# The values of two heads multiplied together on the two halves of the array's columns, with a second buffer of turned weights

## The chip, the cores and the metric

One core of one Trainium2 chip runs the whole kernel, one launch. The metric is the device time of that launch in microseconds (us). The profiled execution is another run of the same program; its own time is given beside the median below.

## What is computed

The reference is one inference step of a two-layer trunk: a gated-linear-attention layer, then a stick-breaking attention layer over shared K and V. It runs for a prompt of 512 tokens and for 8 samples of one token each with 2048 cached positions. What the change touches is the stick-breaking attention of the prompt (16 heads of 64 features), which stands late in the program. Beside it runs the sum over the cached values of the samples.

```python
# one head, a block of queries; k, v: the 512 new tokens
z = q @ k.T * scale + bias
mask = k_pos < q_pos
log_keep = where(mask, log_sigmoid(-z), 0)
later = cumsum(log_keep, reverse=True) - log_keep
a = where(mask, exp(log_sigmoid(z) + later), 0)
o = a @ v                      # then times silu(g), then the output projection
```

## The kernel before

Every engine has its own program written out by hand, and counting semaphores tie them together. The order on an engine is the order in which its block is written; a wait holds up all that stands behind it on that engine.

The stage of the prompt's heads starts at about 802 us and ends at about 949 us of the span. For head h the work runs through the engines like this:

- TensorE, `scores(h)` (L1762): four mask products and four score products into banks 1, 0 and 2; the rows of the array used are 64, the features of one head. It is issued one head ahead.
- ScalarE, `head_sigmoids(h)` (L865): two sigmoids of each bank into `pcum[h % 2]` and `psig[h % 2]`.
- VectorE, `head_products(h)` (L1300): four scans along the keys, then four multiplications. The result, the weights, stands in `psig[h % 2]`; semaphore `a_p`.
- TensorE, `weights_back(h)` (L1778): ten 128x128 transposes of the weights into banks 3, 4 and half of bank 1; semaphore `at_t`.
- VectorE, `head_weights(h)` (L1320): three copies of these banks into the buffer `pat`, the turned weights; semaphore `at_out`.
- TensorE, `values(h)` (L1792): four products of V with `pat`, 1280 columns in all, that fill only 64 of the array's 128 columns; heads of even number write partitions 0 to 63 of bank 5, odd ones 64 to 127; semaphore `o_p`.
- VectorE, `gate_pair(i)` (L1316): one multiplication of bank 5 by the gate, once for two heads; semaphore `u1_out`.

There is one buffer `pat`, so `head_weights(h)` waits for `values(h - 1)`. An fp32 product stands twice in the trace, as two passes.

Between these stands the work of the samples. The cached V has 128 pages of 512 KB. `value_quad(m0)` (L1804) multiplies four pages, each on 32 of the array's 128 columns; the stage holds quads 16 to 31, one for each head. After each fourth quad VectorE masks the sum (`sample_rows`, L1248, semaphore `ob`), TensorE turns it with eight products of one column (`sample_features`, L1820, semaphore `sf_mm`) and VectorE multiplies it in (`sample_gate`, L1256, semaphore `so1_used`). The next quad overwrites the same banks, so it waits for `so1_used`.

The pages are loaded by SyncE (`load_page`, L449). A page of V lies in slot `(n - FEW) % 7` of seven, n the page's number in the order of loading, so the slot of a page comes free when the quad that used the page seven before is done; SyncE waits for that on `v_used`, which counts quads. Of two quads that follow each other, 4 + 4 pages, the last page of the second one lies in the slot of the first page of the first one. It can be issued only when the first quad has ended.

The loop of TensorE at L1850 sets the order: for each head `scores(h + 1)`, `weights_back(h)`, then `value_quad` and `values(h)`; where a quad starts a new sample (h = 0, 4, 8, 12) it is `sample_features`, `values(h)`, `value_quad`.

Of the kernel before, what the change touches and what calls it, by code (L numbers as in the profile page):

```python
# [4 lines left out]
F32 = mybir.dt.float32  # L5
# [7 lines left out]
P = 128  # L13
D = 1024
KT = D // P
NP_TOK = 512
NS = 8
T = NP_TOK + NS
H2 = T // 2
TB = NP_TOK // P  # L20
# [7 lines left out]
SH, HD = 16, 64  # L28
# [60 lines left out]
QUAD = 4  # L89
# [14 lines left out]
NZ = P * (1 + 2 + 3 + 4)  # L104

AB = {0: (3, 0), 1: (4, 0), 3: (4, 384), 2: (1, 256)}
AO = {0: 0, 1: 512, 3: 896, 2: 1024}
# [54 lines left out]
PER_SAMPLE = NPG // QUAD  # L162
# [20 lines left out]
def build(nc, x_prompt, x_sample, state_gla, cache_k, cache_v, page_table, p_prompt, p_sample,  # L183
# [3 lines left out]
    with ExitStack() as ctx:  # L187
# [3 lines left out]
        def at(name, shape, dt, offset):  # L191
            return nc.alloc_sbuf_tensor_at(name, shape, dt, offset=offset)

        def size(shape, dt=F32):
            n = 2 if dt == BF16 else 4
            for s in shape[1:]:
                n *= s
            return (n + 63) // 64 * 64

        def new(name, shape, dt=F32):  # L200
            t = at(name, shape, dt, top[0])
            top[0] += size(shape, dt)
            assert top[0] <= nc.sbuf_usable_end, (name, top[0] - nc.sbuf_usable_end)
            return t
# [57 lines left out]
        offB = off_phase  # L262
# [40 lines left out]
        V1 = new("V1", [P, TB, D])  # L303
# [13 lines left out]
        pz = size([P, NZ + 4])  # L317
        psig = [at(f"psig{i}", [P, NZ], F32, offB + i * pz) for i in range(2)]
        pcum = [at(f"pcum{i}", [P, NZ + 4], F32, offB + (2 + i) * pz) for i in range(2)]
        pat = at("pat", [P, NZ], F32, offB + 4 * pz)  # L320
        w_unsplit = [w_raw[:, 0, :], w_raw[:, 1, :]] + [at(f"w_unsplit{i}", [P, 2048], F32, off_split + i * 8192)[:] for i in range(2)]

        pp = [ctx.enter_context(nc.psum_tensor(f"pp{i}", [P, 2, 512], F32)) for i in range(4)]
        bank = [pp[i // 2][:, i % 2, :] for i in range(8)]
# [9 lines left out]
        def S(name):  # L334
            if name not in sems:
                sems[name] = ctx.enter_context(nc.semaphore(name))
            return sems[name]
# [603 lines left out]
        def _(dve):  # L941
# [230 lines left out]
            for u in range(8):  # L1172
                h = u // 2
# [140 lines left out]
                last.then_inc(S("a_p"), 1)  # L1314

            def gate_pair(i):  # L1316
                dve.wait_ge(S("o_p"), 2 * i + 2)
                nc.vector.tensor_tensor(g1T[:, i, 0:NP_TOK], bank[5], g1T[:, i, 0:NP_TOK], ALU.mult).then_inc(S("u1_out"), 1)

            def head_weights(h):  # L1320

                dve.wait_ge(S("at_t"), h + 1)
                if h:
                    dve.wait_ge(S("o_p"), h)
                for bk, b0, c0, n in ((3, 0, 0, 512), (4, 0, 512, 512), (1, 256, 1024, 256)):
                    last = nc.vector.tensor_copy(pat[:, c0:c0 + n], bank[bk][:, b0:b0 + n])
                last.then_inc(S("at_out"), 1)

            head_products(0)
            for h in range(SH):  # L1330
                quad = 16 + h
                if quad % PER_SAMPLE == 0:
                    sample_rows(quad // PER_SAMPLE - 1)
                if h % 2 == 0 and h:
                    gate_pair(h // 2 - 1)
                head_weights(h)
                if quad % PER_SAMPLE == 0:
                    sample_gate(quad // PER_SAMPLE - 1)
                if h + 1 < SH:
                    head_products(h + 1)  # L1340
            gate_pair(SH // 2 - 1)
            sample_rows(NS - 1)
            sample_gate(NS - 1)
# [33 lines left out]
        def _(pe):  # L1377
# [150 lines left out]
            for k in range(KT):  # L1528
                if k >= 3:
                    pe.wait_ge(S("x_T"), k - 2)  # L1530
                for b in range(TB):
                    last = nc.tensor.transpose(bank[4 + k % 3][:, b * P:(b + 1) * P], xin[:, b, k * P:(k + 1) * P], ident[:])
# [8 lines left out]
            for k in range(KT):  # L1541
                last = nc.tensor.matmul(sB[0:SW, 336:336 + RANK], hsA[:, k % SV, SW * (k // SV):SW * (k // SV + 1)], wgk[:, k, :],
                                        start=(k == 0), stop=(k == KT - 1))
# [10 lines left out]
            for h in range(GH):  # L1554
                last = nc.tensor.matmul(sC[:, 384 + h * NS:384 + (h + 1) * NS], w2[:, h * P:(h + 1) * P], lrT[:, 0:NS],
                                        start=True, stop=True)
# [6 lines left out]
            for h in range(GH):  # L1563
                nc.tensor.matmul(bank[4 + h], w2[:, h * P:(h + 1) * P], sqacc[0:RANK, 0:NP_TOK],
                                 start=True, stop=True).then_inc(S("gk_mm"), 1)
# [120 lines left out]
            for u in range(8):  # L1686
                h = u // 2
# [74 lines left out]
            def scores(h):  # L1762

                i, r = h // 2, (h % 2) * HD
                for e, (bk, _, blocks) in enumerate(ZBANKS):
                    if h:
                        pe.wait_ge(S("sig_p"), (h - 1) * len(ZBANKS) + e + 1)
                    for q in blocks:
                        c0, n = ZB[q][1], (q + 1) * P
                        nc.tensor.matmul(bank[bk][:, c0 + n - P:c0 + n], identb[:], maskneg[:],  # L1770
                                         start=(q != 2), stop=False, skip_group_check=True)
                    for q in blocks:
                        c0, n = ZB[q][1], (q + 1) * P
                        last = nc.tensor.matmul(bank[bk][:, c0:c0 + n], q1T[r:r + HD, i, q * P:(q + 1) * P],  # L1774
                                                K1T[r:r + HD, i, 0:n], start=False, stop=True, skip_group_check=True)
                    last.then_inc(S("z_p"), 1)

            def weights_back(h):  # L1778

                pe.wait_ge(S("a_p"), h + 1)  # L1780
                if h:
                    pe.wait_ge(S("at_out"), h)
                for kb in (0, 1, 3, 2):
                    bk, c0 = AB[kb]
                    if bk == ZBANKS[0][0] and h + 1 < SH:
                        pe.wait_ge(S("sig_p"), (h + 1) * len(ZBANKS) + 1)
                    for q in range(kb, TB):
                        last = nc.tensor.transpose(bank[bk][:, c0 + (q - kb) * P:c0 + (q - kb + 1) * P],  # L1788
                                                   psig[h % 2][:, PSEG[q] + kb * P:PSEG[q] + (kb + 1) * P], ident[:])
                last.then_inc(S("at_t"), 1)  # L1790

            def values(h):  # L1792
                r = (h % 2) * HD
                pe.wait_ge(S("at_out"), h + 1)
                if h >= 2 and h % 2 == 0:
                    pe.wait_ge(S("u1_out"), h // 2)
                for kb in range(TB):
                    n = (TB - kb) * P
                    last = nc.tensor.matmul(bank[5][r:r + HD, kb * P:NP_TOK], V1[:, kb, h * HD:(h + 1) * HD],  # L1799
                                            pat[:, AO[kb]:AO[kb] + n], start=(kb == 0), stop=(kb == TB - 1),  # L1800
                                            skip_group_check=True)
                last.then_inc(S("o_p"), 1)

            def value_quad(m0):  # L1804

                b, j0 = m0 // NPG, m0 % NPG
                e0 = NSB + NPAGES + m0
                for e in range(e0, e0 + QUAD):
                    pe.wait_ge(S(f"slot_in{SLOT_OF[e]}"), 16 * SLOT_TURN[e])
                if j0 == 0 and b:  # L1810
                    pe.wait_ge(S("so1_used"), b)
                for t in range(2):
                    for g in range(QUAD):
                        c = (j0 + g) * P + b * SH
                        last = nc.tensor.matmul(pp[3][32 * g:32 * g + 32, t, :], zs[:, c:c + 32],  # L1815
                                                slot[SLOT_OF[e0 + g]][:, t * 512:(t + 1) * 512],
                                                start=(j0 == 0), stop=(j0 == NPG - QUAD), skip_group_check=True)
                last.then_inc(S("v_used"), 1)

            def sample_features(b):  # L1820

                pe.wait_ge(S("ob"), b + 1)
                for i in range(KT):
                    last = nc.tensor.matmul(bank[6][:, i:i + 1], ob[:, i * P:(i + 1) * P], ones[:, 0:1], start=True, stop=True)  # L1824
                last.then_inc(S("sf_mm"), 1)
# [19 lines left out]
            for t in range(16 - KV_LAG, 16):  # L1845
                kv_transposes(t)

            scores(0)
            pe.wait_ge(S("kv_out"), 16)
            for h in range(SH):  # L1850
                if h + 1 < SH:
                    scores(h + 1)
                weights_back(h)
                if (16 + h) % PER_SAMPLE == 0:
                    sample_features((16 + h) // PER_SAMPLE - 1)
                    values(h)
                    value_quad(QUAD * (16 + h))
                else:
                    value_quad(QUAD * (16 + h))
                    values(h)  # L1860
            sample_features(NS - 1)
            pe.wait_ge(S("so1_used"), NS)

# [51 lines left out]
```

## Time and profile before

| | |
|---|---|
| median of 3 runs | 1101.58 us (1098.48 to 1110.49) |
| the profiled execution's own time | 1100.77 us |
| its span | 1099.0 us |
| mean granted TensorE clock | 0.933 of full |
| TensorE (PE) busy | 963.0 us, 88% of the span |
| VectorE (DVE) busy | 689.0 us, 63% |
| ScalarE (ACT) busy | 308.1 us, 28% |
| GpSimd (POOL) busy | 236.2 us, 21% |
| chain that ended last | PE 53%, DVE 24%, issue 6%, DMA 4%, ACT 3% |

PE is the matmul side of TensorE, PEld its weight loads, SPq what SyncE issues. Ends of matmuls in the trace are modelled: a group's busy time in the timeline reaches a little beyond the start of what follows, so distances between starts are the better measure. In the chain of waits a piece ends where the next one begins.

### The profile page before, as it was taken

How to read it: one execution, taken by the hardware profiler on the slowest of the kernel's cores; microseconds unless marked ns; L12 is line 12 of the kernel's file. 1: busy time of each engine (PE TensorE's matmuls, PEld its weight loads, DVE VectorE, ACT ScalarE, POOL GpSimd, SP SyncE). 2: the span in 40 equal slices, each digit the busy share in tenths (PEclk: the TensorE clock that was granted, in tenths of full speed). 3: DMA queues.
4: the chain of work that ended last, by engine and by line, in shares of the span. 5: the costliest groups of instructions: out<-in, count | busy, mean ns of one | idle time of the engine just before them, and what ended most of it. 6: DMA issues, size and time to landing. Idle time of an engine off the chain costs nothing.

```text
span 1099.0 us, 14307 instructions
## 1 busy us (share of the span) xinstructions
PE 963.0 (88%) x5297; PEld 662.6 (60%) x5297; DVE 689.0 (63%) x807; ACT 308.1 (28%) x495; POOL 236.2 (21%) x131
## 2 busy tenths in 40 slices
PE   6899767779977997998876989999999999799894
PEld 4566536667764443444345868877754444499893
DVE  5553226877757999999997542222167777565554
ACT  5211245323322112121001321111133433233333
POOL 2000004463313555544552020000000000001110
PEclk9999887889979999999998999999989999899997
DMA  7969842543335987787987109887866766322212
GB/s 274 347 228 360 316 166 62 190 142 119 120 96 191 328 309 262 229 287 249 308 289 246 39 20 321 315 306 285 285 215 211 269 222 224 128 78 78 77 39 78
DMA packets 111157, 228.22 MB, mean 208 GB/s; under 512 B 7249, under 2 KB 70328, under 8 KB 111088
## 3 DMA queue, kind: packets, MB, share of 16 engines
q1 hardware_dynamic: 53184, 167.41, 44.0%
q10 hardware_dynamic: 57904, 59.90, 16.5%
q8 instruction: 42, 0.69, 0.3%
q14 instruction: 27, 0.22, 0.1%
HBM read 216.18 MB, written 11.11 MB: 207 GB/s over the span
## 4 chain that ended last, share of the span: by engine, by line
PE 53%; DVE 24%; issue 6%; DMA 4%; ACT 3%; ACTq 0%; POOLq 0%; POOL 0%; SPq 0%; DVEq 0%
PE pp L1443 15%; PE pp L1446 8%; DVE slot L1103 7%; DVE zall L1104 7%; PE pp L1815 6%; PE pp L1429 4%; PE pp L1774 3%; PE pp L1799 3%; DMA w_raw<-in_gla_w_in_dram 3%; PE pp L1788 2%; PE pp L1824 1%; PE pp L1432 1%; PE pp L1673 1%; DVE rstd L978 1%; PE pp L1495 1%
## 5 line engine op out<-in xcount | busy, mean ns | idle before, releaser
L538 POOL TENSOR_TENSOR slot<-slot,qb 128x1024 f32<-128x1024 f32 x78 | 201.4, 2597 | 260.4 <-DMA slot<-in_cache_k_dram 218.1
L950 DVE TENSOR_TENSOR w_lo<-w_raw,w_hi 128x1024 fp32r<-128x1024 f32 x62 | 84.7, 1370 | 116.3 <-ACT w_hi L597 116.3
L1104 DVE TENSOR_REDUCE zall<-slot 128x16 f32<-128x1024 f32 x128 | 151.9, 1213 | 1.7
L1446 PE MATMUL pp<-xa_hi,w_hi 128*128 128x512 f32 x200 | 86.8, 434 | 13.8 <-DVE w_lo L950 13.8
L1432 PE MATMUL pp<-xn,w_unsplit 128*128 128x512 f32 x192 | 86.3, 603 | 6.6 <-DVE q1T L973 6.6
L1103 DVE TENSOR_TENSOR slot<-slot,qb 128x1024 f32<-128x1024 f32 x50 | 89.2, 1784 | 0.0
L597 ACT CAST w_hi<-w_raw 128x1024 fp32r<-128x1024 f32 x62 | 64.4, 1044 | 86.9 <-PE pp L1446 39.7
L1432 PE MATMUL pp<-xn,w_raw 128*128 128x512 f32 x192 | 85.2, 598 | 2.7 <-ACT xn L608 2.7
L1443 PE MATMUL pp<-xb_hi,w_hi 128*128 128x260 f32 x384 | 79.4, 288 | 6.8 <-DVE w_lo L950 5.3
L1446 PE MATMUL pp<-xa_lo,w_hi 128*128 128x512 f32 x200 | 83.2, 416 | 0.0
L1446 PE MATMUL pp<-xa_hi,w_lo 128*128 128x512 f32 x200 | 82.9, 415 | 0.0
L1443 PE MATMUL pp<-xb_lo,w_hi 128*128 128x260 f32 x384 | 77.7, 284 | 0.0
L1443 PE MATMUL pp<-xb_hi,w_lo 128*128 128x260 f32 x384 | 77.6, 284 | 0.0
L526 POOL COPY sqacc<-work 128x520 f32<-128x520 f32 x2 | 1.3, 647 | 349.6 <-ACT work L615 349.6
L1432 PEld LDWEIGHTS pp<-xn,w_unsplit 128*128 128x128 f32 x192 | 36.8, 193 | 52.4 <-issue 52.2
L1815 PE MATMUL pp<-slot,zs 128*32 128x512 f32 x512 | 64.2, 620 | 1.4 <-DVE g1T L1258 1.1
L1443 PEld LDWEIGHTS pp<-xb_hi,w_hi 128*128 128x128 f32 x384 | 59.8, 191 | 8.6 <-DVE w_lo L950 5.7
L1432 PEld LDWEIGHTS pp<-xn,w_raw 128*128 128x128 f32 x192 | 36.8, 192 | 46.6 <-issue 41.9
L1443 PEld LDWEIGHTS pp<-xb_hi,w_lo 128*128 128x128 f32 x384 | 59.6, 190 | 0.0
L1443 PEld LDWEIGHTS pp<-xb_lo,w_hi 128*128 128x128 f32 x384 | 59.6, 190 | 0.0
L1446 PEld LDWEIGHTS pp<-xa_hi,w_hi 128*128 128x128 f32 x200 | 40.8, 204 | 29.6 <-DVE w_lo L950 14.8
L872 ACT ACTIVATE pcum<-pp,nbiasbc 128x256 f32<-128x256 f32 (+1 forms) x64 | 32.4, 532 | 87.5 <-PE pp L1774 86.7
(284 smaller groups left out, 1599.7 us busy)
## 6 DMA issues: line engine op xcount, KB each, us to landing
slot<-in_cache_k_dram SPq DMA_DIRECT2D x128, 512.0 KB, 4.7
slot<-in_cache_v_dram SPq DMA_DIRECT2D x128, 512.0 KB, 5.3
w_raw<-in_gla_w_in_dram ACTq DMA_DIRECT2D x12, 1024.0 KB, 7.4
slot<-in_gla_w_in_dram SPq DMA_DIRECT2D x24, 512.0 KB, 10.5
w_raw<-in_w_kv_dram ACTq DMA_DIRECT2D x8, 1024.0 KB, 10.5
w_raw<-in_w_ple_gate_dram ACTq DMA_DIRECT2D x6, 1024.0 KB, 5.6
s<-in_state_gla_dram SPq DMA_DIRECT2D x1, 4096.0 KB, 28.1
slot<-in_gla_w_out_dram SPq DMA_DIRECT2D x8, 512.0 KB, 8.7
```

Of the source, the lines that this page charges most:

```text
L538: nc.gpsimd.tensor_tensor(slot[s][:], slot[s][:], qb[:, (n // NPG) % 2, :], ALU.mult).then_inc(S("k_mul_pool"), 1)
L597: nc.scalar.copy(hi, raw).then_inc(S("w_hi"), 1)
L950: nc.vector.tensor_tensor(lo, raw, hi.bitcast(F32), ALU.subtract).then_inc(S("w_split"), 1)
L1103: own.then(nc.vector.tensor_tensor(at, at, qb[:, b % 2, :], ALU.mult))
L1104: nc.vector.tensor_reduce(zall[:, n % NPG, b * SH:(b + 1) * SH], at.rearrange("p (h d) -> p h d", d=HD), AX.X, ALU.add).then_inc(S("k_used ...
L1429: last = nc.tensor.matmul(pp[m % 2][:, t, 0:H2], w[:, k, :], x[:, t * H2:(t + 1) * H2], start=(k == 0), stop=(k == KT - 1))
L1432: last = nc.tensor.matmul(bank[m % 2], w[:, k, :], x[:, 0:NP_TOK], start=(k == 0), stop=(k == KT - 1))
L1443: last = nc.tensor.matmul(pp[m % 2][:, t, 0:H2], w[:, k, :], x[:, t * H2:(t + 1) * H2], start=(k == 0 and first), stop=(k == KT - 1 and w ...
L1446: last = nc.tensor.matmul(bank[m % 2], w[:, k, :], x[:, 0:NP_TOK], start=(k == 0 and first), stop=(k == KT - 1 and w is wl))
L1774: last = nc.tensor.matmul(bank[bk][:, c0:c0 + n], q1T[r:r + HD, i, q * P:(q + 1) * P], K1T[r:r + HD, i, 0:n], start=False, stop=True, skip ...
L1799: last = nc.tensor.matmul(bank[5][r:r + HD, kb * P:NP_TOK], V1[:, kb, h * HD:(h + 1) * HD], pat[:, AO[kb]:AO[kb] + n], start=(kb == 0), st ...
L1815: last = nc.tensor.matmul(pp[3][32 * g:32 * g + 32, t, :], zs[:, c:c + 32], slot[SLOT_OF[e0 + g]][:, t * 512:(t + 1) * 512], start=(j0 == ...
```

## The change

`pat` becomes a pair of buffers, one for each head of a pair, in memory that was free. `values` now takes a pair i: it waits until the weights of both heads are copied and issues, for each of the four key blocks, the product of the even head (columns 0 to 63 of the array) and then that of the odd head (columns 64 to 127), each from its own buffer. `o_p` counts pairs, and the waits on it follow; `head_weights(h)` waits only for the pair before. `scores(h)` gets a wait for `at_out`, which `values` used to give it implicitly. In the loop of TensorE `values` stands after every odd head. A quad that starts a new sample no longer follows `sample_features`; it stands one iteration later, after `scores` and before `weights_back`. The products are the same ones in the same number.

```diff
-        pat = at("pat", [P, NZ], F32, offB + 4 * pz)
+        pat = [at(f"pat{i}", [P, NZ], F32, offB + (4 + i) * pz) for i in range(2)]
...
             def gate_pair(i):
-                dve.wait_ge(S("o_p"), 2 * i + 2)
+                dve.wait_ge(S("o_p"), i + 1)
...
             def head_weights(h):
                 dve.wait_ge(S("at_t"), h + 1)
-                if h:
-                    dve.wait_ge(S("o_p"), h)
+                if h >= 2:
+                    dve.wait_ge(S("o_p"), h // 2)
                 for bk, b0, c0, n in ((3, 0, 0, 512), (4, 0, 512, 512), (1, 256, 1024, 256)):
-                    last = nc.vector.tensor_copy(pat[:, c0:c0 + n], bank[bk][:, b0:b0 + n])
+                    last = nc.vector.tensor_copy(pat[h % 2][:, c0:c0 + n], bank[bk][:, b0:b0 + n])
...
             def scores(h):
                 i, r = h // 2, (h % 2) * HD
+                if h >= 2:
+                    pe.wait_ge(S("at_out"), h - 1)
...
-            def values(h):
-                r = (h % 2) * HD
-                pe.wait_ge(S("at_out"), h + 1)
-                if h >= 2 and h % 2 == 0:
-                    pe.wait_ge(S("u1_out"), h // 2)
+            def values(i):
+
+                pe.wait_ge(S("at_out"), 2 * i + 2)
+                if i:
+                    pe.wait_ge(S("u1_out"), i)
                 for kb in range(TB):
                     n = (TB - kb) * P
-                    last = nc.tensor.matmul(bank[5][r:r + HD, kb * P:NP_TOK], V1[:, kb, h * HD:(h + 1) * HD],
-                                            pat[:, AO[kb]:AO[kb] + n], start=(kb == 0), stop=(kb == TB - 1),
-                                            skip_group_check=True)
+                    for e in range(2):
+                        h, r = 2 * i + e, e * HD
+                        last = nc.tensor.matmul(bank[5][r:r + HD, kb * P:NP_TOK], V1[:, kb, h * HD:(h + 1) * HD],
+                                                pat[e][:, AO[kb]:AO[kb] + n], start=(kb == 0), stop=(kb == TB - 1),
+                                                skip_group_check=True)
...
             for h in range(SH):
                 if h + 1 < SH:
                     scores(h + 1)
+                if (15 + h) % PER_SAMPLE == 0:
+                    value_quad(QUAD * (15 + h))
                 weights_back(h)
                 if (16 + h) % PER_SAMPLE == 0:
                     sample_features((16 + h) // PER_SAMPLE - 1)
-                    values(h)
-                    value_quad(QUAD * (16 + h))
                 else:
                     value_quad(QUAD * (16 + h))
-                    values(h)
+                if h % 2:
+                    values(h // 2)
```

The order of TensorE's instructions between the first quad of a sample, quad 20, and the next one, before. `slot4_136` is the buffer of a page, its first number the slot; `zs` holds the samples' weights, `psig1` those of head 5. The last product of quad 20 stands first, then scores(6), the transposes of head 5, and the first product of quad 21:

```order
L1815 MATMUL pp3<-slot0_77,zs_81 32x512
L1770 MATMUL pp0<-maskneg_61,identb_60 128x128
L1774 MATMUL pp0<-K1T_133,q1T_132 128x256
L1770 MATMUL pp0<-maskneg_61,identb_60 128x128 x2
L1774 MATMUL pp0<-K1T_133,q1T_132 128x128
L1774 MATMUL pp0<-K1T_133,q1T_132 128x384
L1770 MATMUL pp1<-maskneg_61,identb_60 128x128
L1774 MATMUL pp1<-K1T_133,q1T_132 128x512
L1788 MATMUL pp1<-ident_58,psig1_150 128x128 x4
L1788 MATMUL pp2<-ident_58,psig1_150 128x128 x4
L1788 MATMUL pp0<-ident_58,psig1_150 128x128 x2
L1815 MATMUL pp3<-slot1_78,zs_81 32x512
```

The same place after the change, from the second half of quad 20 through the transposes of head 5 into quad 21 (L1820 is the quad's line now, L1791 that of the transposes):

```order
L1820 MATMUL pp3<-slot4_136,zs_81 32x512
L1820 MATMUL pp3<-slot5_137,zs_81 32x512
L1820 MATMUL pp3<-slot6_138,zs_81 32x512
L1820 MATMUL pp3<-slot0_77,zs_81 32x512
L1791 MATMUL pp1<-ident_58,psig1_150 128x128 x4
L1791 MATMUL pp2<-ident_58,psig1_150 128x128 x4
L1791 MATMUL pp0<-ident_58,psig1_150 128x128 x2
L1820 MATMUL pp3<-slot1_78,zs_81 32x512
L1820 MATMUL pp3<-slot2_79,zs_81 32x512
L1820 MATMUL pp3<-slot3_80,zs_81 32x512
L1820 MATMUL pp3<-slot4_136,zs_81 32x512
```

The scores are gone from between the two quads; only the ten transposes are left, and both quads use slot 4, for different pages.

TensorE's order around the features of a sample, before: the transposes of head 4, the features, the values of head 4.

```order
L1788 MATMUL pp1<-ident_58,psig0_149 128x128 x4
L1788 MATMUL pp2<-ident_58,psig0_149 128x128 x4
L1788 MATMUL pp0<-ident_58,psig0_149 128x128 x2
L1824 MATMUL pp3<-ones_59,qb_83 128x1 x8
L1799 MATMUL pp2<-pat_153,V1_135 64x512
L1799 MATMUL pp2<-pat_153,V1_135 64x384
L1799 MATMUL pp2<-pat_153,V1_135 64x256
L1799 MATMUL pp2<-pat_153,V1_135 64x128
```

The same place after the change (L1829 the features, L1773 and L1777 the scores of head 6):

```order
L1791 MATMUL pp1<-ident_58,psig0_149 128x128 x4
L1791 MATMUL pp2<-ident_58,psig0_149 128x128 x4
L1791 MATMUL pp0<-ident_58,psig0_149 128x128 x2
L1829 MATMUL pp3<-ones_59,qb_83 128x1 x8
L1773 MATMUL pp0<-maskneg_61,identb_60 128x128
L1777 MATMUL pp0<-K1T_133,q1T_132 128x256
L1773 MATMUL pp0<-maskneg_61,identb_60 128x128 x2
L1777 MATMUL pp0<-K1T_133,q1T_132 128x128
L1777 MATMUL pp0<-K1T_133,q1T_132 128x384
L1773 MATMUL pp1<-maskneg_61,identb_60 128x128
L1777 MATMUL pp1<-K1T_133,q1T_132 128x512
L1820 MATMUL pp3<-slot4_136,zs_81 32x512
```

The values of head 4 and the quad have gone from behind the features; the scores follow at once.

TensorE's values of a pair after the change, heads 4 and 5 (`pat0` and `pat1` are the two buffers of turned weights):

```order
L1804 MATMUL pp2<-pat0_153,V1_135 64x512
L1804 MATMUL pp2<-pat1_154,V1_135 64x512
L1804 MATMUL pp2<-pat0_153,V1_135 64x384
L1804 MATMUL pp2<-pat1_154,V1_135 64x384
L1804 MATMUL pp2<-pat0_153,V1_135 64x256
L1804 MATMUL pp2<-pat1_154,V1_135 64x256
L1804 MATMUL pp2<-pat0_153,V1_135 64x128
L1804 MATMUL pp2<-pat1_154,V1_135 64x128
```

Products of the two heads now alternate, where four of one head stood in a row.

## Rows read from the trace of the kernel before

**Rows 1.** The page: busy us (share of the span) and instructions of each engine.
```profile
PE 963.0 (88%) x5297; PEld 662.6 (60%) x5297; DVE 689.0 (63%) x807; ACT 308.1 (28%) x495; POOL 236.2 (21%) x131
```

**Rows 2.** Busy time in a stretch of four heads: us, engines, clock, DMA, GB/s.
```profile
841.20:877.68 36.48, 36.45 (x201) 17.49 (x201) 27.27 (x50) 13.63 (x29) 0.00 (x0) 1.00 0.68 231
```

**Rows 3.** Chain of waits in order of time, two heads: start us, us, what.
```profile
844.71 1.68 PE pp L1824 x16
...
846.42 2.37 PE pp L1799 x8
848.79 1.85 PE pp L1815 x16
850.65 0.16 PE pp L1770
...
853.93 1.24 PE pp L1788 x10
855.17 1.85 PE pp L1815 x16
857.02 2.30 PE pp L1799 x8
859.32 0.16 PE pp L1770
```

**Rows 4.** Timeline at the last head: start us, us, engine line op [idle before <-releaser].
```profile
936.86 1.62 DVE L1326 COPY pat<-pp 128x512 f32<-128x512 f32 x3 [1.84 <-PE pp L1788]
938.39 2.96 DVE L1307 TENSOR_TENSOR_SCAN pcum<-pcum,ones 128x256 f32<-128x256 f32 x4
...
941.39 1.70 DVE L1313 TENSOR_TENSOR psig<-psig,pcum 128x128 f32<-128x128 f32 x4
943.14 1.31 PE L1788 MATMUL pp<-ident,psig 128*128 128x128 f32 x10 [2.17 <-DVE psig L1313]
...
944.49 1.62 DVE L1326 COPY pat<-pp 128x512 f32<-128x512 f32 x3 [1.41 <-PE pp L1788]
```

**Rows 5.** Instructions by shape, 841.2 to 877.7 us: line, shapes, xcount, busy us, mean ns.
```profile
L1815 PE MATMUL pp<-slot,zs 128*32 128x512 f32 x64 | 7.7, 598 | 0.0
...
L1799 PE MATMUL pp<-pat,V 128*64 128x512 f32 x8 | 4.3, 618 | 0.0
```

**Rows 6.** Timeline around quad 20's end: the loads that it lets go.
```profile
850.85 3.61 SPq L455 DMA_DIRECT2D slot<-in_cache_v_dram  x4
```

**Rows 7.** Loads in 850.8 to 850.9, then in 841 to 878: xcount, KB, us to landing.
```profile
slot<-in_cache_v_dram SPq DMA_DIRECT2D x1, 512.0 KB, 3.5
...
slot<-in_cache_v_dram SPq DMA_DIRECT2D x17, 512.0 KB, 4.8
```

**Rows 8.** Busy time by stretch around three falls of the clock, columns as in rows 2.
```profile
724.50:726.80 2.30, 1.95 (x19) 1.75 (x23) 0.87 (x2) 0.00 (x0) 0.00 (x0) 0.98 0.96 384
726.80:730.10 3.30, 3.30 (x17) 0.72 (x10) 0.00 (x0) 0.00 (x0) 0.00 (x0) 0.50 0.13 49
...
791.90:801.80 9.90, 7.93 (x38) 3.74 (x34) 4.26 (x8) 7.25 (x18) 0.00 (x0) 1.00 0.85 259
801.80:812.00 10.20, 9.63 (x33) 7.16 (x34) 7.23 (x13) 0.71 (x2) 0.00 (x0) 0.50 0.40 164
...
941.00:943.10 2.10, 0.00 (x0) 0.00 (x0) 2.05 (x5) 0.00 (x0) 0.00 (x0) 1.00 1.02 368
...
948.60:952.00 3.40, 1.49 (x15) 1.48 (x14) 1.82 (x2) 0.00 (x0) 0.00 (x0) 1.00 0.00 0
952.00:962.20 10.20, 7.00 (x32) 6.13 (x32) 4.64 (x8) 3.19 (x6) 0.00 (x0) 0.50 0.34 104
```

**Rows 9.** Timeline at head 0, at the low clock: the same groups of TensorE.
```profile
802.37 2.40 PE L1788 MATMUL pp<-ident,psig 128*128 128x128 f32 x10 [1.55 <-DVE psig L1313]
...
804.56 3.41 PE L1824 MATMUL pp<-ones,qb 128*128 128x1 f32 x16
...
807.90 4.41 PE L1799 MATMUL pp<-pat,V 128*64 128x512 f32 x8
```

More of the change, by code:

```diff
@@ L319, in build @@
         pcum = [at(f"pcum{i}", [P, NZ + 4], F32, offB + (2 + i) * pz) for i in range(2)]
-        pat = at("pat", [P, NZ], F32, offB + 4 * pz)
+        pat = [at(f"pat{i}", [P, NZ], F32, offB + (4 + i) * pz) for i in range(2)]
+        assert 6 * pz <= 2 * size([P, KT, T])
         w_unsplit = [w_raw[:, 0, :], w_raw[:, 1, :]] + [at(f"w_unsplit{i}", [P, 2048], F32, off_split + i * 8192)[:] for i in range(2)]
```

## Prediction

> **What bounds the kernel now.** I read the page first: TensorE is busy 88% of the span and VectorE 63% [rows 1]. That is an average, so I then read the busy time of the stage that the change touches. Four heads, with the features of one sample in them, take 36.48 us, and TensorE is busy for 36.45 of them at full clock; VectorE for 27.27 [rows 2]. So TensorE sets the pace here, and the chain of waits shows with what [rows 3]: transposes of a head 1.24 us, a quad 1.85, the values of a head 2.30, and from the first mask product at 850.65 to the transposes at 853.93 the scores, 3.28. That is 8.67 us a head. Each fourth head has the features besides, 1.68. While the quad runs, VectorE copies the turned weights, so the wait of the values for them is nearly nothing.
>
> Next comes the reserve of VectorE. The last head shows its own loop, since there TensorE had to wait [rows 4]: copies from 936.86, scans from 938.39, multiplications from 941.39 for 1.70, transposes from 943.14, the next copies at 944.49. That is 7.63 us from copies to copies, of which the transposes are 1.35. From the end of one head's transposes to the start of the next ones VectorE therefore needs about 6.3 us, whatever TensorE does. Before, TensorE itself needs 1.85 + 2.30 + 3.28 = 7.43 in this place, so 1.1 us are in reserve.
>
> **What the change removes.** The values of a head are eight passes, 2 x (512 + 384 + 256 + 128) = 2560 columns in 2.30 us [rows 3], on 64 of 128 columns of the array. The nearest evidence that tiles side by side run at once is the quad: 16 passes of 512 columns, 8192 in all, on four tiles of 32, in 1.85 us [rows 3]. A quad's product lasts 598 ns by itself and the one of the values 618 [rows 5], so the passes are equally long and four of them run together. I take the same for two tiles of 64 with two sources: a pair costs 2.30 instead of 4.60, which saves 2.3 us, eight times, **-18.4 us**. The bounds are 0 (the tiles follow one another) and this.
>
> The Trainium skill, "TensorE: Matmul & The Clock Gate", Part 3 (Packing small matmuls), speaks for less: it has three column tiles at 2.38 times one. At that efficiency two tiles give 1.59 times, a pair would cost 2.9 us and the saving would be 13.6. The quads here show the full factor, so the row decides and the sum goes on with 18.4.
>
> **What it adds, first: a quad waits for its page.** Two quads used to stand at least 4.5 us apart: quad 20 ends at about 850.6 and quad 21 starts at 855.17 [rows 3]. Now quads 16, 20, 24 and 28 stand ahead of the transposes, and the next quad right behind them. The last page of the second quad lies in the slot of the first page of the first one. SyncE can issue it only when the first quad is done: at 850.85, some 0.2 us after it ended [rows 6], and it lands 3.5 us later [rows 7]. That is about 3.75 us from the end of the quad, and before there was cover for it: 4.5 us. After the change the cover is the transposes, 1.24. What is left, 2.5 us, TensorE stands still, and the values and the next scores stand behind it in its queue. Four times, **+10.0 us**. The load is the first of its group, and the queue has run dry by then (between it and the quad before stand values, scores, transposes, features and scores again, 2.3 + 3.3 + 1.2 + 1.7 + 3.3 = 11.8 us), so the 3.5 us of the first load hold and not the 4.8 of the median of 17 [rows 7]. Bounds: with 4.8 us it is 3.8 each, 15 in all; nothing only if the page landed within 1.2 us of the quad's end, a third of the shortest load in the rows.
>
> **Second: VectorE's loop comes into sight.** Behind an even head no values stand, so from transposes to transposes TensorE has only quad and scores, 1.85 + 3.28 = 5.1, against the 6.3 of VectorE. It waits 1.2 us before heads 3, 7 and 11. Before head 15 there are no more scores either; only the quad is left, and the wait is 4.4 us, where it was 2.17 [rows 4]. Together 3.6 + 2.2 = **+5.8 us**. Where head 0, 4, 8 or 12 comes first, features, scores and quad make 6.8 us, so nothing waits. Behind the odd heads the pair's values stand: 7.4, nothing either. The new wait of the scores for `at_out` costs 0.1 at most: the copies end 1.7 us after the transposes, and quad or features, 1.68, run in that time. The copies of a head no longer wait for anything but the transposes; this gives nothing, as they hardly waited before.
>
> Without the clock the sum against the profiled execution's own 1100.8 us is 1100.8 - 18.4 + 10.0 + 5.8 = **1098.2**. The gain is mostly eaten by waits of its own making. (The median of the runs is 0.8 higher.)
>
> **Third: the clock.** TensorE's clock is at its upper level, 2.4 GHz, from 812 us to the end of the stage; the question is whether it stays there with the new gaps. The falls of this trace show what precedes them [rows 8]. In 724.5 to 726.8 the features of a sample, eight products of one column, stood with a gap of 0.35 us; behind it the clock was 0.50, that is 1.2 GHz, until 730.1. In 948.6 to 952.0 TensorE was idle for over half and then did features; 0.50 until 962.2. In 791.9 to 801.8, transposes and scores with a fifth of idle time, then 0.50 until 812. On the other side, the features of head 4 were followed at once by values and a quad [rows 3], and the clock held [rows 2]; an idle 2.1 us at 941.0 with dense work around it did no harm either. After the change there are nine weaker places: four times features with scores behind them in place of values, four stalls of 2.5 us behind transposes, and 4.4 us of idle time before head 15. No row is just like any of them; they lie between the falls and the non-falls, nearer to the falls, so I take six in ten of the nine, 5.5 falls.
>
> A fall costs half of its length where TensorE is the pace: transposes take 2.40 instead of 1.24, features 3.41 instead of 1.68, values 4.41 instead of 2.37 [rows 9, 3]. Lengths are 3.3 to 10.2 us [rows 8]. Behind a stall stand quad and values, dense work, which speaks for short ones; behind features stand scores, which speaks for longer ones. I take 5.4 us, so 2.7 a fall: 5.5 x 2.7 = **+15 us**. Bounds: no fall, 0; all nine, 24.
>
> Sum: 1098.2 + 15 = 1113.
>
> **The rivals.**
> - *The clock holds* (at most two falls). For it: 941.0, and that no gap is longer than 2.5 us but one. Against it: 724.5. Then 1098 to 1104, no change that could be measured. Chance 0.17.
> - *The pages are in time and the clock falls seldom; this one ends on the other side.* If the first quad's slots came free early, or a load took under 1.3 us, no stall would arise: 1100.8 - 18.4 + 5.8 = 1088, and the four stalls would be gone as places of falls too. It decides at 1.24 us from the end of a quad to the landing, against 3.75 in the rows. Chance 0.08.
> - *No stall of the pages, but falls behind the features and at head 15*: 1092 to 1100. Chance 0.10.
> - *The two halves do not overlap.* Each product waits for the one before it though its tile is free, and the change does not do what it says. The -18.4 is gone, the waits for VectorE shrink little, the stalls stay: 1112 and up to 1125 with falls. Against it: the quads, four tiles at once. Chance 0.07.
> - *The forecast*: halves overlap, stalls of the pages, three to eight falls: 1106 to 1122. Chance 0.58.
>
> **How the numbers follow.** 1113 us is the forecast's own value. The forecast and the rivals on its upper side leave little above 1122; below, 1088 alone is left out, with the lower end of the third rival: 1095 to 1122. About 1% is what a measurement of this kernel can tell from no change: below 1091 lies the second rival and some of the third, 0.11; above 1112.6 lies over half of the forecast and most of the fourth rival, 0.42; the rest is 0.47.
>
> **What would show it.** In the profile after, the values' line should have its 128 instructions, starting in twos, and a pair lasting about 2.3 to 2.4 us; starts one behind the other speak for the halves not overlapping. Before quads 17, 21, 25 and 29 TensorE should be idle for 2.5 us, released by a load of V's pages; if there is no such idle time, the second term is wrong. Transposes of heads 3, 7 and 11 should show 1.2 us of waiting for VectorE, and head 15 4.4. The granted clock from 812 to 950 us should show stretches at 0.50, after features or stalls. A clock of 1.00 throughout makes it 1098, and the third term wrong. Nothing ahead of 800 us should move by more than its scatter.

## The result: 1.0% slower

The changed kernel takes 1117.34 us in the median of 20 runs (1108.95 to 1125.65), the kernel before 1106.26 in 20 runs (1098.48 to 1114.55). The ratio is 1.0101, 95% interval 1.0074 to 1.0128. The profiled execution took 1117.59 us with a span of 1115.9, against 1100.77 and 1099.0 before.

The two spans differ by 16.9 us, but not all of this belongs to the change. The stage of the heads began at 802.37 us before and at 805.36 after, and from its end to the end of the program 150.3 to 150.4 us passed in both. Ahead of the stage the programs are the same, and its begin lay between 802 and 811 us in all the runs of this study. So I read the length of the stage, from the start of the first transposes to the start of VectorE's last gate multiplication. These rows are the busy time by stretch of that stage, columns as in [rows 2]. First before:

```profile
802.37:948.64 146.27, 143.97 (x776) 70.41 (x776) 103.87 (x183) 47.87 (x99) 0.00 (x0) 0.97 0.64 219
```

Then the same of the changed kernel, and under it the stretches in which its clock was low:

```profile
805.36:965.58 160.22, 143.25 (x776) 68.36 (x776) 104.22 (x184) 48.21 (x99) 0.00 (x0) 0.85 0.58 200
...
805.36:822.00 16.64, 16.64 (x63) 10.01 (x63) 7.44 (x13) 3.65 (x8) 0.00 (x0) 0.50 0.24 91
839.00:842.40 3.40, 3.15 (x14) 2.20 (x18) 0.91 (x3) 0.46 (x1) 0.00 (x0) 0.50 0.95 347
852.70:862.90 10.20, 10.20 (x32) 3.68 (x33) 4.48 (x8) 3.52 (x7) 0.00 (x0) 0.50 0.00 0
866.30:869.70 3.40, 3.40 (x16) 0.71 (x10) 3.37 (x6) 0.00 (x0) 0.00 (x0) 0.50 0.88 336
897.00:900.40 3.40, 3.40 (x18) 0.59 (x16) 1.84 (x5) 1.95 (x4) 0.00 (x0) 0.50 0.00 0
934.60:938.00 3.40, 3.40 (x17) 0.59 (x16) 1.65 (x4) 1.63 (x3) 0.00 (x0) 0.50 0.00 0
941.40:944.80 3.40, 2.78 (x16) 0.68 (x16) 3.37 (x7) 0.00 (x0) 0.00 (x0) 0.50 0.88 307
958.50:961.90 3.40, 3.40 (x18) 2.35 (x22) 1.01 (x2) 0.00 (x0) 0.00 (x0) 0.50 0.05 15
```

The stage is 14.0 us longer, with the same 776 matmul passes. TensorE's busy time hardly changed, 143.97 to 143.25, though 18 us of products now run beside each other: the low clock put back what the pairs took away. Seven new stretches at 1.2 GHz stand in the list, and the one at the start is longer, 16.6 us in the stage against 9.6 before [rows 8]. Together 47.2 us are low, where 9.6 were. Those are two profiles; the clock of every run says the same of the whole program. Over the 20 runs of the changed kernel it is 0.913 in the mean, over the 23 runs of the kernel before beside experiments e5 to e8 it is 0.926. That makes about 195 against 163 us at the low clock, 32 more.

The chain of waits, in order of time, shows a pair and its surroundings (start us, us, what):

```profile
837.71 1.50 DVE psig L1314 x3
839.25 2.40 PE pp L1791 x10
841.65 2.24 PE pp L1820 x16
843.89 2.31 PE pp L1804 x16
846.20 0.16 PE pp L1773
```

An fp32 product is two passes, so these are eight products: sixteen passes of two heads in 2.31 us, where eight passes of one head took 2.30 [rows 3]. The halves do overlap, fully. In front of them VectorE released the transposes (L1791), which run at the low clock, 2.40 us instead of 1.24.

The timeline around the first quad of a sample, TensorE's and SyncE's rows:

```profile
858.27 3.64 PE L1820 MATMUL pp<-slot,zs 128*32 128x512 f32 x16
...
861.84 1.80 PE L1791 MATMUL pp<-ident,psig 128*128 128x128 f32 x10
862.12 8.54 SPq L456 DMA_DIRECT2D slot<-in_cache_v_dram  x6
...
865.66 3.06 PE L1820 MATMUL pp<-slot,zs 128*32 128x512 f32 x16 [2.02 <-DMA slot<-in_cache_v_dram]
```

The first load is issued at 862.12, the quad that needs it starts 3.54 us later, 2.02 of them idle. The summary of waits in the stage (engine line, who it waited for: us in total, times, longest) has the two kinds:

```profile
PE pp L1791 <- DVE psig L1314: 9.6, 5, 4.5
PE pp L1820 <- DMA slot<-in_cache_v_dram: 8.8, 4, 2.5
```

Before, the first of them was 3.7 us in 2 times, and the second was not there:

```profile
PE pp L1788 <- DVE psig L1313: 3.7, 2, 2.2
```

### The profile page after: what moved, and what is told of

It is laid out like the page before. It is cut to its first block, busy times and chain, and to the rows that moved or that the text cites. A ratio compares the mean times of both kernels' runs of the same rounds, so it can differ in the third digit from the quotient of the medians.

```text
span 1115.9 us, 14320 instructions
## 1 busy us (share of the span) xinstructions
PE 966.9 (87%) x5297; PEld 663.2 (59%) x5297; DVE 689.1 (62%) x807; ACT 308.4 (28%) x495; POOL 237.0 (21%) x131
## 4 chain that ended last, share of the span: by engine, by line
PE 51%; DVE 25%; issue 6%; DMA 5%; ACT 3%; ACTq 0%; POOLq 0%; POOL 0%; SPq 0%; DVEq 0%
PE pp L1444 14%; PE pp L1447 8%; DVE slot L1104 7%; DVE zall L1105 7%; PE pp L1820 6%; PE pp L1430 4%; PE pp L1777 3%; DMA w_raw<-in_gla_w_in_dram 3%; PE pp L1433 2%; DMA slot<-in_cache_v_dram 2%; PE pp L1804 2%; PE pp L1791 2%; PE pp L1829 1%; PE pp L1674 1%; DVE pcum L1308 1%
## 5 line engine op out<-in xcount | busy, mean ns | idle before, releaser
L1820 PE MATMUL pp<-slot,zs 128*32 128x512 f32 x512 | 73.6, 699 | 10.1 <-DMA slot<-in_cache_v_dram 8.9
```

## The experiments

All ratios are against the kernel before, run beside each experiment on the same chip, with their 95% interval. They are not the quotient of two medians and can differ from it by some tenths of a per cent. Stage lengths and stretches at the low clock come from one profile each. A short account serves for all of them: stage = 146.3 us of before, minus 18.4 for the pairs, plus the additional idle time of TensorE, plus half of the additional time at the low clock.

**The quad ahead of the scores.** This takes the wait for the page away by leaving more work between the two quads.

```diff
             for h in range(SH):
-                if h + 1 < SH:
-                    scores(h + 1)
                 if (15 + h) % PER_SAMPLE == 0:
                     value_quad(QUAD * (15 + h))
+                if h + 1 < SH:
+                    scores(h + 1)
                 weights_back(h)
```

> The changed kernel with one step moved: the quad that starts a sample stands ahead of the scores, not behind them, so scores and transposes (3.3 + 1.2 = 4.5 us) lie between it and the next quad, more than the 3.5 to 3.8 us from its end to the landing of its page. Theory (pages and clock): no idle time before quads 17, 21, 25 and 29, -10 us; the features are followed by a quad, so fewer of the seven low stretches of the clock between 816 and 973 us, -5 to -11; a short wait for the sample's gate, +1. Against the changed kernel -15 to -20 us, so 0.985 to 0.99 of the kernel before. Rival (the idle time before the quads only takes the place of waits that come anyway, for VectorE, and the pair costs what it saves): no gain over the changed kernel, 1.01.

Measured: 1103.54 us, ratio 0.9971 (0.9942 to 1.0000). The stage takes 145.9 us, 14.3 less than in the changed kernel. Its waits:

```profile
PE pp L1791 <- DVE psig L1314: 9.6, 5, 4.5
...
PE pp L1820 <- DVE g1T L1259: 1.4, 4, 0.4
```

No load holds TensorE any more; the gate of the samples costs 1.4 us in four times. The direction and the mechanism are as expected, and so are the terms: 8.8 us of waits for pages gone, 1.4 added, and 13.3 us less at the low clock, of which half is 6.6. That makes 14.0, and 14.3 were measured, a little under the 15 to 20 that I gave. The ratio that I gave, 0.985 to 0.99, doesn't follow from that: 15 to 20 us off 1.0101 are 0.992 to 0.997. What stays low, apart from the start:

```profile
805.54:951.42 145.88, 136.39 (x776) 66.24 (x776) 103.95 (x183) 48.05 (x99) 0.00 (x0) 0.88 0.64 219
880.50:883.90 3.40, 3.40 (x16) 0.59 (x13) 3.37 (x7) 0.00 (x0) 0.00 (x0) 0.50 0.00 0
904.40:907.80 3.40, 3.40 (x20) 0.94 (x18) 2.61 (x6) 0.00 (x0) 0.00 (x0) 0.50 0.63 249
918.00:928.20 10.20, 10.20 (x34) 4.53 (x26) 3.61 (x6) 3.52 (x7) 0.00 (x0) 0.50 0.62 204
941.90:948.70 6.80, 5.40 (x26) 2.59 (x26) 2.96 (x6) 0.00 (x0) 0.00 (x0) 0.50 0.25 86
```

Two of these begin behind features (880.5, 918.0), with a quad behind the features and not scores; two begin at a wait for VectorE (904.4, 941.9).

**One head after the other.** Only the order of the eight products is changed.

```diff
-                for kb in range(TB):
-                    n = (TB - kb) * P
-                    for e in range(2):
+                for e in range(2):
+                    for kb in range(TB):
+                        n = (TB - kb) * P
```

> The changed kernel with the eight products of a pair in another order: all four of the even head, then all four of the odd one, nothing else moved. Theory: the two halves of the columns ran at once only because the products alternate; now the pair takes 4.6 instead of 2.3 us, eight times, +18 us, a little less where a wait for VectorE or a page hides behind it: 1.02 to 1.028 of the kernel before. Rival 1 (the queue looks far enough ahead to overlap them anyway): pair 2.3 us, 1.01 as the changed kernel. Rival 2 (VectorE is the pace now, the values are hidden): pair 4.6 us but 1.01.

Measured: 1142.04 us, ratio 1.0315 (1.0290 to 1.0340), and a stage of 180.9 us, 20.6 more than with alternating products. So the order makes the overlap, and the values are not hidden behind VectorE. The result is above the expected 1.02 to 1.028 although the pair takes less than 4.6 us. Timeline of TensorE:

```profile
843.45 3.93 PE L1804 MATMUL pp<-pat,V 128*64 128x512 f32 x16
847.31 0.23 PE L1773 MATMUL pp<-maskneg,identb 128*128 128x128 bf16 x1
```

From the first product to the next mask it is 3.86 us: the odd head's first pass starts at 845.01, beside the last two products of the even head. Against 2.31 that is 12.4 us in eight pairs. The rest is the clock: the granted share in the stage is 0.81, against 0.85, which is 20 us more at the low clock and 10 us by the account. The waits for pages are 0.9 us shorter. Together that is 22, a little more than the 20.6 measured.

**The quad moved alone**, in the kernel before:

```diff
                     scores(h + 1)
+                if (15 + h) % PER_SAMPLE == 0:
+                    value_quad(QUAD * (15 + h))
                 weights_back(h)
                 if (16 + h) % PER_SAMPLE == 0:
                     sample_features((16 + h) // PER_SAMPLE - 1)
                     values(h)
-                    value_quad(QUAD * (16 + h))
```

> The kernel before with the moved quad alone: the values of each head by themselves with one buffer, but the quad that starts a sample stands behind the next scores and ahead of the transposes. Theory: before quads 17, 21, 25 and 29 TensorE is idle for 2.3 to 2.5 us with a load of a page as the releaser, +10 us, and some of these gaps bring the clock down, two falls of 2.7: +5; together 1.009 to 1.015 of the kernel before. Rival (the stall appears only because the pair made TensorE faster): 1.00, no idle time before these quads.

Measured: 1120.62 us, ratio 1.0136 (1.0104 to 1.0168). The stall needs no pair:

```profile
PE pp L1815 <- DMA slot<-in_cache_v_dram: 10.4, 4, 2.7
```

Busy time of the stage:

```profile
811.00:974.36 163.36, 150.65 (x776) 72.46 (x776) 104.31 (x183) 47.94 (x99) 0.00 (x0) 0.93 0.56 196
```

The stage is 163.4 us, 17.1 more than before: 10.4 of idle time, and 23.0 us at the low clock instead of 9.6, of which half is 6.7. The sum is 17.1.

**The gaps filled.** The changed kernel, with products that write into bank 5 what `values` overwrites; they do no work of use, and TensorE's waits get no shorter by them.

```diff
+            def fill(h, columns):
+                pe.wait_ge(S("u1_out"), h // 2)
+                for n in columns:
+                    nc.tensor.matmul(bank[5][:, 0:n], ident[:], V1[:, 0, 0:n], start=True, stop=True, skip_group_check=True)
...
+                if h % 4 == 3:
+                    fill(h, (512,) * 5 if h == SH - 1 else (512, 128))
                 weights_back(h)
...
                 else:
+                    if h % 4 == 1:
+                        fill(h, (512, 512, 256))
                     value_quad(QUAD * (16 + h))
```

> The changed kernel with TensorE kept busy in its waits: products of the identity with V into bank 5, which values overwrites; 1280 columns before quads 17, 21, 25 and 29 (2.1 us of the 2.5), 640 before the transposes of heads 3, 7 and 11 (1.1 of 1.2) and 2560 before those of head 15 (4.3 of 4.4). No wait gets shorter and no useful work is gone. Theory (the clock is the third term): the low stretches behind the gaps vanish, those behind features with scores stay, so three to five of seven fewer, -8 to -13 us against the changed kernel: 0.998 to 1.004 of the kernel before. Rival (the idle time itself is all the cost, the clock falls elsewhere or costs nothing): 1.01 or more, since the filling can only delay.

Measured: 1113.94 us, ratio 1.0058 (1.0026 to 1.0089), against the changed kernel's 1.0101 (1.0074 to 1.0128). That is 0.4% faster, but the intervals overlap; the stage is 155.8 us, 4.4 less. Half of what I had expected as the least. What remains low, apart from the start:

```profile
851.90:858.70 6.80, 6.80 (x23) 1.95 (x23) 3.64 (x6) 3.36 (x7) 0.00 (x0) 0.50 0.01 2
892.90:896.30 3.40, 3.40 (x17) 0.59 (x16) 1.59 (x4) 1.55 (x3) 0.00 (x0) 0.50 0.00 0
927.00:937.20 10.20, 10.16 (x31) 3.54 (x32) 4.74 (x9) 3.52 (x7) 0.00 (x0) 0.50 0.00 1
```

All four falls behind gaps have gone (839, 866, 941 and 958 in the changed kernel), and all three behind features with scores have stayed. So the number of falls is what I expected; their price is not. I had counted 5.4 us of low clock for each, and the four that went had been 3.4 us long; the three that stayed are 20.4 us together, where they were 17.0. From the start of the features to each of the three that stayed TensorE was idle for no more than 0.04 us. So idle time is one cause, as far as one profile against another can show it, and features with what stands behind them are another that needs none. The one at 927.0 begins as the features end, before the scores have done anything.

**Ahead of the scores, and the waits filled.** The kernel of the first experiment, with the filling before heads 3, 7, 11 and 15 alone (the first of the two insertions above).

> The kernel of e1 (the quad ahead of the scores) with TensorE kept busy while it waits for VectorE: 640 columns of filling products before the transposes of heads 3, 7 and 11 and 2560 before those of head 15, into bank 5, which values overwrites. In e1 the clock fell at 880.5 and 918.0, behind features, and at 904.4 and 941.9, behind such waits. Theory (idle time brings the clock down): the two falls behind waits go, those behind features stay; 3 to 6 us less than e1, 0.992 to 0.995 of the kernel before. Rival (the falls of e1 come from the scores, which use half of the rows, and not from the waits): as e1, 0.997.

Measured: 1097.87 us, ratio 0.9917 (0.9884 to 0.9950). The stage is 136.5 us, 9.4 less than without the filling, though the same useful instructions wait for the same things:

```profile
808.74:945.19 136.45, 134.98 (x798) 66.56 (x798) 103.93 (x184) 47.95 (x99) 0.00 (x0) 0.96 0.67 234
```

One profile may overstate it (the ratios differ by 0.54%, some 6 us, and their intervals overlap at the edge), but the clock's share went from 0.88 to 0.96 and only one short fall is left besides the start. It begins at 916.5, behind features and with a quad behind them. Both falls behind waits have gone, as expected; of the two behind features, which I expected to stay, one has gone too.

**A copy on ScalarE.** The kernel of the first experiment; `at_out` now counts two for each head, and the waits for it are doubled.

```diff
-                for bk, b0, c0, n in ((3, 0, 0, 512), (4, 0, 512, 512), (1, 256, 1024, 256)):
+                for bk, b0, c0, n in ((3, 0, 0, 512), (1, 256, 1024, 256)):
...
+                act.wait_ge(S("at_t"), h + 1)
+                if h >= 2:
+                    act.wait_ge(S("o_p"), h // 2)
+                nc.scalar.copy(pat[h % 2][:, 512:1024], bank[4]).then_inc(S("at_out"), 1)
```

> The kernel of e1 with one of the three copies of the turned weights, 512 of the 1280 columns, on ScalarE at the same time as VectorE does the other two, so VectorE's loop is 0.57 us shorter. Theory (VectorE's loop is the second term): the wait before heads 3, 7 and 11 falls from 1.3 to 0.7 us and the one before head 15 from 4.5 to 3.9, 2.4 us in all, and falls of the clock behind them get rarer: 2 to 6 us less than e1, 0.991 to 0.995 of the kernel before. Rival (the copies are not on the path behind even heads, or ScalarE is later than VectorE was): as e1, 0.997 or above.

Measured: 1099.23 us, ratio 0.9923 (0.9893 to 0.9953), stage 138.7 us. This is 7.2 us less than in the first experiment. The wait for VectorE fell by the 2.4 us expected; most of the rest is the clock, whose share rose from 0.88 to 0.92:

```profile
PE pp L1795 <- DVE psig L1318: 7.2, 5, 3.9
```

**All of it together**: the kernel before this one, filling products in every wait of TensorE in the stage (640 columns before the transposes of head 0, 128 before quads 16, 20, 24 and 28, 256 before heads 3, 7 and 11, 2048 before head 15).

> The kernel of e6 with filling products in every wait of TensorE in the stage: 640 columns before the transposes of head 0, 128 before quads 16, 20, 24 and 28, 256 before the transposes of heads 3, 7 and 11, 2048 before those of head 15. Theory: pair, pages, VectorE's loop and clock are the four terms; with the pages in time, 3 us of waits and hardly a fall of the clock the stage takes 146.3 - 18.4 + 3.6 + 1.2 - 5 (the low stretch at its start) = 128 us and the kernel 0.983 to 0.987 of the one before. Rival (something else, such as switching between tile sizes, holds the stage at about 140 us): 0.993 to 0.997.

Measured: 1086.49 us, ratio 0.9814 (0.9782 to 0.9847), 1.9% faster than the kernel before, just beyond the 0.983 to 0.987 that I gave, and 2.8% faster than the changed one. The stage is 128.5 us, where 128 was expected, with the clock never low in it:

```profile
810.67:939.13 128.46, 128.07 (x798) 62.98 (x798) 94.36 (x167) 56.10 (x115) 0.00 (x0) 1.00 0.71 249
```

**The start filled in the kernel before**: nothing but the 640 columns before the transposes of head 0.

> The kernel before with nothing but 640 columns of filling products while TensorE waits for the first transposes (1.1 of 1.5 us idle at 801 us). It measures a fall of the clock by itself, with no pair, page or copy involved. Theory: the low stretch at 801.8 to 812.0 goes or begins later; it costs half of its length where TensorE sets the pace, up to 5 us: 0.995 to 0.998. Rival (the low clock there is hidden, VectorE sets the pace at the start of the stage): 1.000.

Measured: 1101.39 us, ratio 0.9984 (0.9957 to 1.0010), which can't be told from no change. In its profile the first transposes take 1.31 us instead of 2.40 [rows 9] and the low stretch at the start is gone; but two short falls stand elsewhere in the stage, at 841.7 and 940.7, where before had none, and the stage is 145.1 us instead of 146.3. The account gives 144.8, but the difference is too small to test the price. The order of instructions there is that of before, so the falls are partly a matter of chance. The one at 841.7 stands right behind the features of head 4. The chain of waits, then the busy time of the low stretch:

```profile
839.90 1.68 PE pp L1824 x16
841.61 4.06 PE pp L1799 x8
...
841.70:845.10 3.40, 3.40 (x6) 1.14 (x7) 3.37 (x7) 0.00 (x0) 0.00 (x0) 0.50 0.00 0
```

Behind the features (L1824) stand the values of the head (L1799), TensorE is not idle, and the clock falls all the same; the values take 4.06 us instead of 2.37. So values behind the features do not always keep the clock up.

**All of it, one head after the other.** The kernel of e7 with the product order of e2.

> The kernel of e7 with the eight products of a pair in the order of e2: four of the even head, then four of the odd. It takes the overlap of the halves away where the clock holds and pages and VectorE wait for little. In e2 the pair took 3.9 us from its first product to the mask of the next scores, against 2.3 with alternating products, since the odd head's first passes still started beside the even head's last ones. Theory: 8 x 1.55 = 12.4 us more than e7, the stage 141 us, 0.992 to 0.995 of the kernel before, hardly a fall of the clock. Rival (the pair costs 4.6 when nothing else waits): 18 us more, 0.998.

Measured: 1100.22 us, ratio 0.9942 (0.9911 to 0.9973). The stage:

```profile
803.09:943.96 140.87, 140.49 (x798) 68.99 (x798) 94.70 (x167) 56.13 (x115) 0.00 (x0) 1.00 0.65 228
```

140.9 minus 128.5 is 12.4 us, eight times 1.55, with the clock at 1.00 in both. This is the cleanest measure of what the order does; against two heads by themselves (2.30 twice) the overlap is worth 2.3 us a pair.

**Two copies on ScalarE.** The kernel of e7 with 768 of the 1280 columns copied there, and no filling before heads 3, 7 and 11.

> The kernel of e7 with two of the three copies (768 of 1280 columns) on ScalarE, so VectorE's loop is another 0.5 us shorter, and no filling before heads 3, 7 and 11. VectorE then needs 5.2 us from transposes to transposes where TensorE has 5.1 of its own work. Theory: 0.6 us less before heads 3, 7 and 11 and 0.5 before head 15, 2 us less than e7: 0.978 to 0.981 of the kernel before. Rival (ScalarE's two copies, 1.1 us and its later start, now hold up the scores and the values): 0.981 to 0.985.

Measured: 1084.93 us, ratio 0.9805 (0.9764 to 0.9846). The stage is 127.1 us, 1.3 less than in e7; the ratio can't be told from that one's. I had expected 2 us less. By its median this is the fastest kernel of the study, 2% faster than before.

## Why the prediction was right

The forecast was 1113 us on a base of 1100.8, that is 12.2 us more, from the case that I held likeliest. The medians of 20 runs differ by 11.1 us; the profiled stage by 14.0. The median of the kernel before rose from 1101.58 us in three runs to 1106.26 in twenty, so 1117.3 is about the forecast's difference on a base 4.7 us higher. Term by term, in the profile of the changed kernel:

- **The pairs, -18.4: right.** A pair takes 2.31 us for 16 passes. The quads, from which I took the factor, were the right row. The Trainium skill, "TensorE: Matmul & The Clock Gate", Part 3, has 2.38 times for three column tiles. By that efficiency a pair would cost an estimated 2.9 us, which this trace does not bear out: two tiles give the full factor of two.
- **The pages, +10.0: right, 8.8 measured.** The first two of the four were shorter, 1.8 and 2.0 us, since their transposes ran partly at the low clock and covered more; the other two were the 2.5 forecast. The quad moved alone had 10.4.
- **VectorE's loop, +5.8: right, 9.6 - 3.7 = 5.9 measured.** The wait fell by 2.4 us when a copy was taken away from VectorE.
- **The clock, +15: the right cause and about the right size, the size in part by luck.** Counted from the stage it is 160.2 - 146.3 + 18.4 - 8.8 - 5.9 = 17.6 us, for 37.6 more us at the low clock; that is about half of them, as I had priced it. I had taken nine places with six chances in ten each. Of the three places with features and scores after the start all fell (852.7, 897.0, 934.6); of the stalls, two of four (866.3, 941.4); the wait of head 15 did; and so did the one before head 3 (839.0), 1.2 us, which I had not counted as a place. The falls were more than forecast, seven for 5.5, and shorter, 4.4 us in the mean for 5.4. Together they are 30.6 us of low clock, worth 15.3, so the two errors cancel. The other 7.0 us come from the stretch at the start, 16.6 us for 9.6, worth 3.5; the forecast had no term for it. In pricing a fall I also set 3.41 us of one view against 1.68 of another for the features; within the chain of waits it is 3.20 (807.97 less 804.76) against 1.68, still nearly twice.

What remains open is what makes the clock fall behind features. I had taken it that values behind them kept it up before the change. The features of heads 4, 8 and 12 in all twelve profiles can be counted, three in each. With scores behind them (the changed kernel, e2, e4) a fall followed in nine of nine. With a quad behind them (e1, e5, e6) it was five of nine, with 128 filling columns and then a quad (e7, e9, e10) none of nine, and with values (before, e3, e8) one of nine. So what stands behind matters, but scores are not needed for a fall and values are no sure guard. The features are eight products of one column and the scores use 64 of the 128 rows. Which of these properties counts, and how much the moment decides at which a group runs, wasn't taken apart here.

The account holds beyond this kernel. With the pairs at 18.4 us and waits as measured it gives:

- The filled gaps, with the waits of the changed kernel: 146.3 - 18.4 + 8.8 + 5.9 + 13.4 = 156.0 (measured 155.8).
- The quad ahead of the scores: 146.3 - 18.4 + 1.4 + 5.9 + 12.1 = 147.3 (145.9).
- The same with the waits filled, 1.2 in place of 12.1 for the clock: 136.4 (136.5).
- Everything together, with the waits of e6 and no low clock: 146.3 - 18.4 + 1.4 + 3.5 - 4.8 = 128.0 (128.5).

Where much of the low clock coincides with waits for VectorE, it overstates.

Of the rivals, the one on the other side (pages in time, the clock held, 1088 us) describes what the change could have been: with the quad ahead of the scores, a copy on ScalarE and the gaps filled the kernel took 1086. Pages in time were not enough for it: with the quad ahead of the scores alone it was 1103.5, since the clock still fell. That the halves might not overlap fell with the 2.31 us of a pair, and with e2 and e9, where the order alone cost 12.4 us.

## What to carry to other kernels

Before moving a step to a new place in a queue, count the time between it and the next user of the same buffers: here 1.2 us of cover stood where the reload needs 3.7. When work of a busy engine is taken away or moved, look at what now stands behind its thinnest stretches: here scores came to stand behind the features in place of values, and the clock fell nine times in nine instead of one in nine. Products without use in a gap can pay for themselves: filling the waits brought the ratio from 0.9971 to 0.9917 (e1 and e5).

## What was not expected of the hardware

- Two 64-column tiles overlapped only as far as the order of the queue let them: with four products of one tile in a row, the other tile's first pass started 1.56 us after the first (845.01 against 843.45), when the even head's third product began, not at once.
- Half-speed stretches began where TensorE was never idle: behind one-column products, with products on half of the rows (851.90 and 927.00 in the kernel with filled gaps, busy 6.80 of 6.80 and 10.16 of 10.20 us there and without a wait ahead), and once with the values of a head (841.70 in e8, busy 3.40 of 3.40 us).
- The same instructions ahead of the stage took 802 to 811 us in the twelve profiles, and most of this goes with the clock. The kernel before (802.4 us) has 110 us at the low clock ahead of the stage, e6 (811.3 us, the longest) has 134: 24 us more low clock for 9 us more time. Why the clock differs there between runs of the same instructions stays open.
